# Time mixing: GpSimd scales and adds the modulation weights, two instructions for each, in place of VectorE

## The reference, cut to what matters

```
mod_all = jnp.einsum('bd,lde->lbe', jax.nn.silu(c), ada_w) + ada_b[:, None, :]
shift1, scale1, gate1, shift2, scale2, gate2 = jnp.split(mod_all[i], 6, axis=-1)
...
r_h, k_h, v_h, w_h, a_h = heads(r), heads(k), heads(v), heads(decay), heads(a)
y = _rwkv7_scan(r_h, w_h, k_h, v_h, kk, a_h)
```

## Time and profile before

| what | value |
|---|---|
| median of 3 runs | 2780.48 us (2777.47 to 2780.62) |
| the profiled execution | 2787.33 us, its span 2785.7 us |
| busy: PE, DVE, ACT, POOL | 96%, 71%, 46%, 2% of the span |
| time mixing, from the first load of its rows to the next phase | 437.9 to about 787 us |

### The profile page before, as it was taken

One profiled execution on the slowest core, in us unless ns is written; L12 is line 12 of the kernel. 1 busy time (PEld: TensorE's weight loads), 2 busy tenths in 40 slices (PEclk: granted clock), 3 DMA queues, 4 the chain that ended last, 5 costly groups with the idle time before them and its releaser, 6 DMA issues.

```text
span 2785.7 us, 54580 instructions
## 1 busy us (share of the span) xinstructions
PE 2663.9 (96%) x20513; PEld 2288.4 (82%) x20513; DVE 1974.9 (71%) x2611; ACT 1288.5 (46%) x1970; POOL 45.1 (2%) x89
## 2 busy tenths in 40 slices
PE   7899998889889999999999999998989999999998
PEld 2488887888877888888888878887878888888887
DVE  5678845788768777777777876676887655565556
ACT  2355545445444444444444454444454444444444
POOL 1000002000000000000000000000000000000000
PEclk9899999999999999999999999998999999999999
DMA  9889848444366888888888668754878666666653
GB/s 328 309 273 310 301 150 292 131 154 135 120 200 212 287 277 289 286 277 272 281 281 286 230 196 285 231 181 165 280 235 285 230 191 188 190 189 189 186 169 121
DMA packets 486748, 640.15 MB, mean 230 GB/s; under 512 B 23701, under 2 KB 429626, under 8 KB 469946
## 3 DMA queue, kind: packets, MB, share of 16 engines
q1 hardware_dynamic: 482746, 625.32, 68.1%
q0 software_dynamic: 3840, 12.59, 1.2%
HBM read 623.14 MB, written 14.68 MB: 229 GB/s over the span
## 4 chain that ended last, share of the span: by engine, by line
PE 66%; DVE 3%; ACT 1%; issue 1%; DVEq 0%; ACTq 0%
PE ps L1950 42%; PE ps L1954 21%; PE ps L1551 1%; DVE wlo L1934 1%; PE ps L1544 1%; ACT whi L1929 1%; DVE nt L132 1%; DVE act L145 0%; DVE ada_acc L2005 0%; PE ps L1578 0%; PE ps L1586 0%; PE ps L1535 0%; DVE nt L1692 0%; PE ps L2020 0%; PE ps L1568 0%
## 5 line engine op out<-in xcount | busy, mean ns | idle before, releaser
L1934 DVE TENSOR_TENSOR wlo<-raw,whi 128x1024 fp32r<-128x1024 f32 (+1 forms) x768 | 904.2, 1193 | 475.6 <-ACT whi L1929 473.8
L1950 PE MATMUL ps<-act,whi 128*128 128x512 f32 x3784 | 1192.5, 396 | 6.5 <-issue 5.2
L1929 ACT ACTIVATE whi<-raw 128x1024 fp32r<-128x1024 f32 (+1 forms) x768 | 779.3, 1031 | 669.3 <-PE ps L1954 666.4
L1954 PEld LDWEIGHTS ps<-act,wlo 128*128 128x128 f32 x3784 | 712.4, 188 | 168.5
L1954 PE MATMUL ps<-act,wlo 128*128 128x256 f32 x3784 | 744.9, 278 | 0.0
L1950 PE MATMUL ps<-hid,whi 128*128 128x512 f32 x2176 | 680.7, 394 | 8.2 <-DVE wlo L1934 7.2
L1950 PEld LDWEIGHTS ps<-act,whi 128*128 128x128 f32 x3784 | 577.8, 189 | 12.3 <-issue 12.1
L1954 PEld LDWEIGHTS ps<-hid,wlo 128*128 128x128 f32 x2176 | 410.3, 189 | 89.7
L1954 PE MATMUL ps<-hid,wlo 128*128 128x256 f32 x2176 | 433.3, 279 | 0.0
L1950 PEld LDWEIGHTS ps<-hid,whi 128*128 128x128 f32 x2176 | 332.4, 189 | 11.9 <-DVE wlo L1934 7.8
L2005 DVE SCALAR_TENSOR_TENSOR ada_acc<-ada_ring,sc,ada_acc 128x2048 f32<-128x2048 f32 x128 | 300.3, 2346 | 0.3
(11 more groups left out here) (291 smaller groups left out, 2241.9 us busy)
## 6 DMA issues: line engine op xcount, KB each, us to landing
raw<-in_f_w SPq DMA_DIRECT2D x480, 512.0 KB, 4.6
ada_ring<-in_ada_w SPq DMA_DIRECT2D x140, 1024.0 KB, 7.5
raw<-in_a_w_rkv SPq DMA_DIRECT2D x96, 512.0 KB, 5.4
ada_ring<-in_ada_w SPq DMA_DIRECT2D x128, 256.0 KB, 3.2
raw<-in_b_w_in SPq DMA_DIRECT2D x56, 512.0 KB, 4.1
raw<-in_f_w SPq DMA_DIRECT2D x64, 384.0 KB, 4.0
first_ring<-in_ada_w SPq DMA_DIRECT2D x20, 1024.0 KB, 10.8
raw<-in_a_w_o SPq DMA_DIRECT2D x32, 512.0 KB, 7.2
```

The lines of the kernel that those rows point to most:

```text
L1929: self.nc.scalar.activation(self.whi[:, u % SPL, 0:n], self.raw[:, u, 0:n], ACT.Copy).then_inc(self.s("hi_ready"), 1)
L1934: self.nc.vector.tensor_tensor(self.wlo[:, u % SPL, 0:n], self.raw[:, u, 0:n], self.whi[:, u % SPL, 0:n].bitcast(F32), SUB).then_inc(self. ...
L1950: self.nc.tensor.matmul(self.ps[0:c1 - c0, banks[b], :], hi[:, kk, c0:c1], src[:, k].rearrange("p a t -> p (a t)"), start=k == 0, stop=False)
L1954: last = self.nc.tensor.matmul(self.ps[0:c1 - c0, banks[b], T:2 * T], lo[:, kk, c0:c1], src[:, k, 0, :], start=False, stop=k == ktotal - 1)
```

## The change

POOL gets a stream of its own in time mixing, `rows`, with all 8 x 16 operations in order, and DVE loses its calls. Row 0 is one multiply on POOL. Rows 1 to 15 are each two instructions: a multiply in place in the ring (`row` times `sc[:, n]`), a wait for its own semaphore `row_weighed`, and an add of `row` to `ada_acc`. What each waits for is otherwise as before, and SP's stream and PE's are not touched. All of DVE's calls of `adas` go: those of stage N, of stage C, and the one ahead of round 0; of these the diff below shows three.

```diff
 class Stage:
-    has_pool = False
-    def __init__(self, sync, scalar, vector, tensor):
+    has_pool = True
+    def __init__(self, sync, scalar, vector, tensor, pool):
...
-        def ada_op(dve, i, n):
+        def ada_op(pool, i, n):
             u = n // PER
-            dve.wait_ge(s(f"row_loaded{n % 8}"), i * 32 + 16 * (n // 8 + 1))
+            pool.wait_ge(s(f"row_loaded{n % 8}"), i * 32 + 16 * (n // 8 + 1))
             if n == 0:
-                wait(dve, "ada_summed", i + sums0)
+                wait(pool, "ada_summed", i + sums0)
             else:
-                dve.wait_ge(s("ada_row"), i * KT + n)
+                pool.wait_ge(s("ada_row"), i * KT + n)
             acc = self.ada_acc[:, 0:W]
             row = self.ada_ring[:, u % 2, (n % PER) * W:(n % PER + 1) * W]
             if n == 0:
-                last = nc.vector.tensor_scalar(acc, row, self.sc[:, n:n + 1], None, MUL)
+                last = nc.gpsimd.tensor_scalar(acc, row, self.sc[:, n:n + 1], None, MUL)
             else:
-                last = nc.vector.scalar_tensor_tensor(acc, row, self.sc[:, n:n + 1], acc, MUL, ADD)
+                nc.gpsimd.tensor_scalar(row, row, self.sc[:, n:n + 1], None, MUL).then_inc(s("row_weighed"), 1)
+                pool.wait_ge(s("row_weighed"), i * (KT - 1) + n)
+                last = nc.gpsimd.tensor_tensor(acc, acc, row, ADD)
             last.then_inc(s("ada_row"), 1)
+
+        def rows(pool):
+            for i in range(L):
+                for n in range(KT):
+                    ada_op(pool, i, n)
...
-                adas(i, 9, 10, 11, 12)
...
-                    if prep:
-                        adas(i + 1, c)
...
-            adas(0, 0, 1, 2, 3)
...
-        return Stage(sync, scalar, vector, tensor)
+        return Stage(sync, scalar, vector, tensor, rows)
```

More of the change, by code:

```diff
@@ L1719 @@
 class Stage:
-    has_pool = False
-    def __init__(self, sync, scalar, vector, tensor):
-        self.sync, self.scalar, self.vector, self.tensor = sync, scalar, vector, tensor
+    has_pool = True
+    def __init__(self, sync, scalar, vector, tensor, pool):
+        self.sync, self.scalar, self.vector, self.tensor, self.pool = sync, scalar, vector, tensor, pool
 class Program:
@@ L2484, in grow @@
                     tt(name, R[j]["W"][:], R[j]["W"][:], heads4(bank(j, b)), op)
-            def adas(i, *ns):
-                for n in ns:
-                    ada_op(dve, i, n)
             def stage_N(i, q, post, prep):
@@ L2493, in stage_N @@
                     prep_a(i + 1)
-                adas(i, 4)
                 keys(i)
@@ L2498, in stage_N @@
                         prep_b(i + 1, j)
-                adas(i, 5)
                 grow(i, "P2", 1, ADD, "P1")
-                adas(i, 6, 7)
                 grow(i, "P3", 1, ADD, "P2")
-                adas(i, 8)
                 grow(i, "P4", 3, ADD, "P3")
@@ L2511, in stage_N @@
                     prep_c(i + 1, 1 - q)
-                adas(i, 13, 14, 15)
                 grow(i, "W64", 3, SUB, "W32")
```

## The result

The changed kernel takes 2873.81 us (median of 4 runs, 2870.41 to 2874.49), the one before 2779.18 (4 runs). The ratio is 1.0331, 95% interval 1.0318 to 1.0344. The forecast was slower, 2858 us in a range of 2795 to 2950. The profiled execution took 2874.49 us, 87.2 more than that of before.

What follows compares the result with a forecast made beforehand. POOL's chain becomes the bound: 10.2 us in round 0 plus 7 x 7.7 is 64, plus 13 of SBUF contention is 77 us, on 2780.5 about 2858 us for the median, range 2795 to 2950.

Steps and rivals of the forecast that it cites:

- DVE's relief, 2 us a round: Time mixing: of 11.7 us a round taken off DVE, about 2 us a round are worth anything to the chain.
- The two places: Behind DVE's wait for input loads: a multiply-add of 0.73 us stands in its way, one of a few such places.
- POOL's prices: POOL on 512 columns, scaled from 64 and 128: multiply 1.63 us, add 1.23 us.
- the select of 0.90 us: Other bound for POOL's multiply, from a one-input select: 0.90 us for 512 columns, sixteen operations then 35.3 us.
- The chain: POOL's sixteen operations a round, 47.0 us, plus 1.3 bound the round at 48.3 us, 7.7 more than 40.56.
- gaps between them: Between POOL's instructions: each that waits for the one before starts about 0.08 us after its end.
- sum and restart: Between rounds: PE's sum to the bias add 1.09 us, POOL's restart 0.1 to 0.2, together 1.3 us.
- POOL held up by DVE: POOL starting during DVE's two-SBUF-input instructions waits half their length: 1.7 us a round, 13 us in eight.
- Start and end: Round 0's bias add comes 10.2 us later, at 497.6; after round 7's sum nothing changes.
- DVE and POOL in SBUF: Contention for SBUF reads: 1.7 us a round taken, bounds nothing to 43; DVE's other instructions as long as before.
- the full lock: Rival: POOL and DVE instructions stop each other, 63 us a round, 2960 us; in full or part 2885 to 2975, 0.30.
- The rival that POOL is fast enough: POOL's multiply under 1.08 us, so POOL doesn't bound the round: 14 us gain, 2765 us, chance 0.15.

Runs made afterwards that it cites:

- e1: Kernel before without the arithmetic of the time-mixing rows on any engine, DVE still waiting and signalling for each row: 2771.05 us, ratio to before 0.9965.
- e8: Kernel before, all rows on DVE, with row 4 moved ahead of the scan of tile 0 and row 5 between the two scans: 2778.82 us, 0.9994.
- e6: e1 plus 215 POOL adds, no multiplies, on columns nobody reads, for which nothing waits: 2862.39 us, ratio to before 1.0298.
- e5: e1 plus 100 POOL pairs of multiply and add on columns nobody reads, for which nothing waits: 2789.45 us, ratio to before 1.0036.
- e2: Changed kernel with rows 12 to 15 of each round not computed on POOL, only waited for and signalled: 2788.22 us, ratio to before 1.0029.
- e4: Changed kernel with only rows 0 to 7 of each round on POOL, rows 8 to 15 on DVE: 2795.35 us, ratio to before 1.0053.
- e10: As e4, but only rows 0 to 3 of each round on POOL and the rest on DVE: 2787.87 us, ratio to before 1.0028.
- e7: e1 plus 175 POOL multiplies, no adds, on columns nobody reads, for which nothing waits: 2768.64 us, ratio to before 0.9961.
- e9: Changed kernel with two sums used in turn and POOL's multiply of the next row issued ahead of the add: 2831.74 us, ratio to before 1.018.

## Why the prediction was right, and where it was off

**DVE's relief, 2 us a round.** Right in kind, and about half the size when all is counted: 9 us in all by e1's median, though 2.0 us a round between the two profiles. The two places that I named for it are not shown to be the source (e8).

**POOL's prices.** Scaled from 64 and 128 columns to 512 they held: the multiply 1.63 forecast, 1.56 undisturbed; the add 1.23 forecast, 1.27. The line through two narrow rows of the same operation was the better guide than the select of 0.90 us, and a scalar from a tile cost nothing more that shows. The Trainium skill, "GPSIMD Engine Reference", § 3.1, has 769 ns for 512 elements in its best loop, and more for each element of a two-input `tensor_tensor`; the plain multiply here takes twice the 769, and more than the two-input add (1.56 against 1.27 us), so the order is the other way round. The measurement decides.

**The chain.** Right, and the heart of it. Forecast 48.3 us and 1.7 of contention, 50.0 a round; measured 51.24. The step that was short is the sum of its small terms:

| term, us a round | forecast | measured |
|---|---|---|
| 31 instructions, undisturbed | 44.5 | 44.0 |
| gaps between them | 2.5 | 3.8 |
| sum and restart | 1.3 | 2.1 |
| POOL held up by DVE | 1.7 | 1.2 |

The instructions were 16 x 1.63 + 15 x 1.23 and came as 16 x 1.562 + 15 x 1.267 (medians), 44.0; POOL's busy time is 45.2 a round (361.8 / 8), so 1.2 is the held-up part, and 45.2 + 3.8 + 2.1 = 51.1. I had taken 0.08 us for each gap from the earlier trace rows; before a multiply it is 0.17. And I took the sum at full clock: after PE's wait of 8.97 us the granted clock is 0.50, and the sum takes 1.87 us. Seven rounds of 1.24 are 9 of the 10 us by which 77 fell short of 87 between the profiled executions. The rest of the way to 94.6, between medians, is that the profiled execution of before lay some 8 us above its median and that of after within 1 us of its own.

**Start and end.** Round 0 was forecast 10.2 + 1.7 us later and was 12.0. Behind round 7, as forecast, nothing changed.

**DVE and POOL in SBUF.** Here my reasoning was weak. From one overlap of 0.17 us I held blocking to be small, and expected DVE's other instructions to be as long as before. They are not: `be` takes 1.49 us, and DVE's busy time fell by 24 us where the prediction has 93. "SBUF — State Buffer", § Who interferes with whom, in the Trainium skill says that such a pair contends for an exclusive lock, and for POOL's adds the traces here agree (1.30 and 1.41 us from start to start in e6). For its multiplies the traces differ from a lock held for the whole instruction: some 0.55 of 1.56 us. My rival priced the full lock at 63 us a round; e6, with adds all the time, took 61.3, in part by luck, as the rival was worked out for pairs and has no term for TensorE's clock of 0.80. In the changed kernel it changes nothing in the time but POOL's own 1.2 us, since behind all its stops DVE still waits 7 to 16 us at each sum; that cover is POOL's chain, and e5 shows what stands behind it.

**The rival that POOL is fast enough** fell with the price of the multiply, and would probably have been wrong in sign even so: in rounds 1 to 3 of e2, e4 and e10 DVE waits about 0.3 us for the sum, as before, and all three are slower than before.

## What to carry to other kernels

Before work goes to an idle engine, add up its chain between the two points where others wait for it, with every gap and the restart, and hold that against the pitch of the loop: here 49 + 2 against 40.6. Ask what the relieved engine was worth to the path, which here was 9 us for 93 us of work. And count the receiver's two-input instructions, as each may stop a VectorE instruction with two SBUF inputs for nearly its whole length.

## What the runs showed of the hardware that I had not expected

- GpSimd's multiply by a per-partition scalar on 128 x 512 f32 takes 1.56 us, longer than its two-input add of 1.27.
- Beside GpSimd, VectorE's instructions with two SBUF inputs wait for the end of an add, but only for the first 0.55 us or so of a multiply (e6, e7). 175 multiplies beside the recurrence cost nothing that can be measured. VectorE's one-input multiply from SBUF (`k`, 0.41 us before) becomes longer too: 0.78 at the start of a multiply, and 0.70 when begun 1.0 us into one (e7). Its instructions that read PSUM and one SBUF input are as before (`W<-W,ps`, 419 ns against 417).
- A GpSimd instruction that follows directly on the one it waits for starts 0.17 us (a multiply) or 0.08 us (an add) after its end in the changed kernel; with another instruction between them, the gap is gone (e9, 27 us in the kernel).
